# Attention transfers over all 128 partitions, outputs stored ahead of values, gate products later

## The chip, the cores and the metric

The kernel runs on one core of a Trainium2 chip. The metric is the device time of one execution in microseconds (us); lower is better. The profile is one execution recorded by the hardware profiler.

## The reference, cut to what matters

One layer of a diffusion backbone, for 2048 latent tokens and 256 context tokens of width 1024. An input projection yields q, k, v, a gate z_a, the inputs of a convolution branch, a gate z_b and two merge gates. Branch A is attention over a window of the latent grid plus context keys, 8 heads of width 64:

```
q, k, v, z_a, glu, z_b, gates = split(h @ w_in + b_in)
y_a = attend(q, k, v) * silu(z_a)
y_b = conv_branch(glu, ...) * silu(z_b)
g_a, g_b = split(sigmoid(gates))
m = g_a * (y_a @ w_proj_a) + g_b * (y_b @ w_proj_b)
return x + gate * (m @ w_out), k, v
```

Everything is float32. The kernel splits each factor of a product into a high and a low part, so that one product is three matmuls.

## The kernel before, in words

The program has three stages, one after another on TensorE: the input projection (the front), attention over the 8 heads, and the merge with the output projection (the tail). Results of the front go to DRAM (`proj`, `q_hi`, `q_lo`, `k_hi`, `k_lo`, `v`), and the attention loads them head by head.

A head has 18 tiles of 128 queries (`TPH`), so there are `NT` = 144 tiles. For a tile, TensorE forms the scores (`scores`), VectorE adds the bias and takes the minimum (`soften`), ScalarE takes exponents (`exponents`), TensorE transposes them (`turn_probs`) and for each pair of tiles multiplies by the values (`weigh_values`); VectorE multiplies the result by z_a and the inverse of the sum (`gate_out`).

The tiles that a head needs are doubled in SBUF (`n % 2`). `q_sp` (q_split in the profile) has the high part of q in partitions 0 to 63 and the low part in 64 to 127; `k_hi` and `k_lo` have the same 64 rows in both halves, so that one matmul over 128 partitions sums q_hi·k and q_lo·k. `z_sb` and `y_sb` (z_halves, y_halves) hold half of the tokens of a head in the lower 64 partitions and the other half in the upper 64.

All of these transfers are issued by SyncE (SP), in the order of its program. For heads 2 to 7 it issues `load_window` (8 transfers of 16 rows for the bias tables), `load_qk` (6), `load_z` (6), `load_v` (18) and `store_y` of head n - 2 (6). Each load waits until the head two before has let go of the buffer: `load_qk` for `s_mm` (scores done), `load_z` for `y_done`, `load_v` for `pv_done`. What is loaded for head 0 is issued during the front, between the stores of its last units (`load_first`).

```
        for n in range(2, HEADS):
            load_window(sp, n)
            load_qk(n)
            load_z(n)
            load_v(n)
            for part in range(3):
                store_y(sp, n - 2, part)
```

In the tail, `M_UNITS` lists the merge units; those of token chunk 0 (16 units of 256 tokens) come first. VectorE takes each unit out of its PSUM bank, multiplied by its gate (`g_done`), and TensorE may be six units ahead. Between them stand the operations of the convolution branch: `silu_pair` (ScalarE), `gate_yb` (VectorE, times z_b), `yb_high` (ScalarE) and `yb_low` (VectorE), for pairs 0, 1 and 2 of token tiles. Pair 0 belongs to chunk 0, pairs 1 and 2 to chunk 1, which begins with unit 16. z_b of pair 1 (`zb_second`) is loaded at the beginning of the tail.

Of the kernel before, what the change touches and what calls it, by code (L numbers as in the profile page):

```python
# [106 lines left out]
def modulation(nc, io, cst, hT_hi, hT_lo):  # L107
# [80 lines left out]
    io.gate = nc.dram_tensor("gate_rows_dram", (2, D), F32, kind="Internal").ap()  # L188
    io.q_hi, io.q_lo = (nc.dram_tensor(f"q_{h}_rows", (WA, TOK), F32, kind="Internal").ap() for h in ("hi", "lo"))
    io.k_hi, io.k_lo = (nc.dram_tensor(f"k_{h}_rows", (WA, KW), F32, kind="Internal").ap() for h in ("hi", "lo"))  # L190
# [747 lines left out]
def attend(nc, io, cst):  # L938
# [96 lines left out]

    def y_rows(n, half, part):

        rows = slice(DH * n, DH * n + DH)
        if part == 2:
            return rows, slice(LAT + P * half, LAT + P * half + P), slice(LAT // 2, LAT // 2 + P)  # L1040
        at = LAT // 2 * part + 512 * half
        return rows, slice(at, at + 512), slice(512 * part, 512 * part + 512)

    def store_y(sp, n, part):

        sp.wait_ge(y_done, PPH * n + Y_PARTS[part][1])
        for half in range(2):
            rows, tok, at = y_rows(n, half, part)
            sp.dma_start(io.ya[rows, tok], y_sb[DH * half:DH * half + DH, n % 2, at]).then_inc(y_out[n % 2], 16)

# [3 lines left out]
    def wait_y_stored(sp):  # L1054
        for u in range(2):
            sp.wait_ge(y_out[u], 96 * HEADS // 2)

# [15 lines left out]
    def _(sp):  # L1073
        def load_qk(n):

            if n >= 2:
                sp.wait_ge(s_mm, TPH * (n - 1))
            u, rows = n % 2, slice(DH * n, DH * n + DH)
            for half in range(2):
                part = slice(DH * half, DH * half + DH)  # L1080
                sp.dma_start(q_sp[u][part].bitcast(F32), (io.q_hi, io.q_lo)[half][rows]).then_inc(qk_in[u], 16)
                sp.dma_start(k_hi[u][part].bitcast(F32), io.k_hi[rows]).then_inc(qk_in[u], 16)
                sp.dma_start(k_lo[u][part].bitcast(F32), io.k_lo[rows]).then_inc(qk_in[u], 16)

# [28 lines left out]
        def load_z(n):  # L1113
            if n >= 2:
                sp.wait_ge(y_done, PPH * (n - 1))
            for half in range(2):
                for part in range(3):
                    rows, tok, at = y_rows(n, half, part)
                    src = io.proj[ZA0:ZA0 + WA][rows, tok]
                    sp.dma_start(z_sb[DH * half:DH * half + DH, n % 2, at], src).then_inc(z_in[n % 2], 16)  # L1120

# [8 lines left out]
        for n in range(2, HEADS):  # L1130
            load_window(sp, n)
            load_qk(n)
            load_z(n)
            load_v(n)
            for part in range(3):
                store_y(sp, n - 2, part)
        for done in (s_mm, pv_done, red):
            sp.wait_ge(done, TPH * (HEADS - 1))
# [4 lines left out]
        store_y(sp, HEADS - 1, 0)  # L1143
        sp.wait_ge(y_out[0], 96 * HEADS // 2)
        sp.wait_ge(y_out[1], 96 * (HEADS // 2 - 1) + 32)
        tail_stage.load_ya(sp, 0)
# [6 lines left out]
    def _(pe):  # L1153
        def scores(m):

            n, i = BODY[m]
            if m % TPH == 0:
                pe.wait_ge(qk_in[n % 2], 96 * (n // 2 + 1))
            if m >= 2:
# [85 lines left out]
    def _(dve):  # L1245
# [39 lines left out]
        def gate_out(k):  # L1285

            n, at = divmod(k, PPH)
            if at == 0:
                dve.wait_ge(z_in[n % 2], 96 * (n // 2 + 1))
                if n >= 2:  # L1290
                    dve.wait_ge(y_out[n % 2], 96 * (n // 2))
            dve.wait_ge(pv_done, 2 * k + 2)
# [29 lines left out]
    def _(act):  # L1322
# [33 lines left out]
        for m in range(NT + 1):  # L1356
            if 1 <= m < NT - 1:
                exponents(m + 1)
            if m < NT:
                copy_rest(m)  # L1360
                if m % 2:
                    spread(m // 2)
            tail_stage.early_act(act, m)
# [68 lines left out]
def tail(nc, io, cst):  # L1432
# [349 lines left out]
    def yb_high(act, lt):  # L1782

        src, c, tok = yb_parts(lt)
        act.wait_ge(yb_done, yb_count(lt))
        act.activation(y_hi[c][:, 4:8, tok], src, ACT.Copy).then_inc(yb_hid, 1)
# [37 lines left out]
    def tail_act(act):  # L1824
        for n, (c, o, branch) in enumerate(M_UNITS):
            s = n % 16
            if n == 1:
                yb_high(act, 2)
                silu_pair(act, 2)
            if n == 5:  # L1830
                yb_high(act, 4)
            if c == 4 and branch:
# [85 lines left out]
    def tail_dve(dve):  # L1918
        for n, (c, o, branch) in enumerate(M_UNITS):
# [21 lines left out]
            elif og > 32:  # L1941
                m_low(dve, og - 33)
            if n in (0, 4):
                gate_yb(dve, 2 + n // 2)
            if n in (2, 6):
                yb_low(dve, 2 if n == 2 else 4)
            for lt, a, b in turns(c):
# [72 lines left out]
    def early_dve(dve, m):  # L2020
# [10 lines left out]
        if m == NT:  # L2031
            gate_yb(dve, 0)
            yb_low(dve, 0)

    def early_act(act, m):
        for lt, d in pair_steps(m):
# [6 lines left out]
        if m == NT - 3:  # L2043
            ya_high(act, 0, 0)
            ya_high(act, 0, 1)
        if m == NT - 1:
            silu_pair(act, 0)
        if m == NT:
# [12 lines left out]
    T.early_pe, T.early_act, T.early_dve, T.early_pool = early_pe, early_act, early_dve, early_pool  # L2061
    T.lin_done = lin_done
    T.load_first, T.load_wp, T.load_ya = load_ln_first, load_wp, load_ya
# [80 lines left out]
```

## Time and profile before

| | us |
|---|---|
| median of 3 runs (1872.67 to 1877.26) | 1874.98 |
| the profiled execution | 1877.82 |
| its span, first to last instruction | 1875.6 |
| TensorE busy | 1829.8 (98%) |
| VectorE busy | 1015.1 (54%) |
| ScalarE busy | 542.0 (29%) |

The kernel is almost all TensorE. In the table "busy" is the time in which an engine has an instruction running; the rest of TensorE's span, 45.8 us, is idle time in all. The front takes the first 1150 us, attention ends at about 1460 us, the tail takes the rest.

### The profile page before, as it was taken

The numbers are of one execution on the slowest core, as the hardware profiler recorded it, in microseconds if no ns is written. First come the engines' busy times: TensorE is split into PE (matmuls) and PEld (weight loads), VectorE is DVE, ScalarE is ACT, GpSimd is POOL, SyncE is SP. The second block draws the span as 40 slices with busy tenths as digits, with TensorE's granted clock in tenths as the row PEclk, the third lists the DMA queues.
The fourth block names the chain that finished last, engine by engine and source line by source line (L and its number), as shares of the span: only waits on it lengthen the run. The fifth ranks groups of instructions, "written<-read, shape, count | busy, mean of one in ns | idle before, by whom it ended". The sixth has DMA issues, their size and how long they took to land.

```text
span 1875.6 us, 27263 instructions
## 1 busy us (share of the span) xinstructions
PE 1829.8 (98%) x10723; PEld 1561.1 (83%) x10723; DVE 1015.1 (54%) x1710; ACT 542.0 (29%) x1061; POOL 122.8 (7%) x205
## 2 busy tenths in 40 slices
PE   6999999999999999999999999999999899999998
PEld 3788899988888888888888888888888888888886
DVE  3544512111098338816870996766768555654444
ACT  3731101021111111211110114667768222322221
POOL 0100000000000000000000004322330000000000
PEclk9999999999999999999999999999999999999999
DMA  9524423143022112211220164997887767653321
GB/s 318 169 89 158 144 68 132 49 140 115 12 78 89 65 34 82 76 40 59 72 80 20 65 153 119 211 178 163 175 182 176 229 205 244 193 191 140 141 101 56
DMA packets 211145, 235.08 MB, mean 125 GB/s; under 512 B 47707, under 2 KB 157131, under 8 KB 207819
## 3 DMA queue, kind: packets, MB, share of 16 engines
q1 hardware_dynamic: 210760, 233.24, 42.5%
q8 instruction: 85, 1.39, 0.3%
q14 instruction: 41, 0.34, 0.1%
q10 hardware_dynamic: 259, 0.11, 0.0%
HBM read 152.52 MB, written 80.78 MB: 124 GB/s over the span
## 4 chain that ended last, share of the span: by engine, by line
PE 90%; SPq 4%; DMA 2%; issue 1%; ACT 1%; DVE 1%; POOLq 0%; DVEq 0%; POOL 0%; ACTq 0%
PE banks L789 17%; PE banks L790 17%; PE banks L791 17%; PE banks L1742 4%; PE banks L1741 4%; PE banks L1743 4%; PE banks L1713 3%; PE banks L1715 3%; PE banks L1714 3%; PE banks L1225 3%; SPq L1093 2%; PE banks L784 2%; PE banks L785 2%; PE banks L786 2%; PE banks L1191 2%
## 5 line engine op out<-in xcount | busy, mean ns | idle before, releaser
L789 PE MATMUL banks<-h_hi,w_hi 128*128 128x512 f32 (+1 forms) x1600 | 593.3, 371 | 3.6 <-DVE h_lo L598 2.5
L790 PE MATMUL banks<-h_lo,w_hi 128*128 128x512 f32 (+1 forms) x1600 | 589.4, 368 | 0.0
L791 PE MATMUL banks<-h_hi,w_lo 128*128 128x512 f32 (+1 forms) x1600 | 589.3, 368 | 0.0
L730 DVE SCALAR_TENSOR_TENSOR conv_acc<-glu_out,taps,conv_acc 128x773 f32<-128x773 f32 x360 | 371.5, 1032 | 12.3
L789 PEld LDWEIGHTS banks<-h_hi,w_hi 128*128 128x128 f32 x1600 | 301.8, 189 | 57.6 <-issue 3.4
L791 PEld LDWEIGHTS banks<-h_hi,w_lo 128*128 128x128 f32 x1600 | 301.8, 189 | 50.7
L790 PEld LDWEIGHTS banks<-h_lo,w_hi 128*128 128x128 f32 x1600 | 302.0, 189 | 49.0
L506 ACT ACTIVATE out_stage<-banks,param_cols 128x512 f32<-128x512 f32 (+1 forms) x120 | 77.0, 647 | 439.2 <-PE banks L791 433.2
L1713 PE MATMUL banks<-y_hi,wp_hi 128*128 128x512 f32 (+1 forms) x320 | 120.0, 375 | 4.9 <-DVE m_sum L1935 2.8
L1332 ACT ACTIVATE probs<-scores,stat 128x640 f32<-128x640 f32 (+2 forms) x128 | 106.7, 834 | 60.2 <-DVE stat L1259 58.6
L1715 PE MATMUL banks<-y_hi,wp_lo 128*128 128x512 f32 (+1 forms) x320 | 118.4, 370 | 0.0
L1714 PE MATMUL banks<-y_lo,wp_hi 128*128 128x512 f32 (+1 forms) x320 | 118.3, 370 | 0.0
L1742 PE MATMUL banks<-wo_lo,mo_hi 128*128 128x512 f32 x288 | 112.9, 392 | 0.0
L1741 PE MATMUL banks<-wo_hi,mo_hi 128*128 128x512 f32 x288 | 112.7, 391 | 0.0
L1743 PE MATMUL banks<-wo_hi,mo_lo 128*128 128x512 f32 x288 | 112.5, 391 | 0.0
L1259 DVE CUSTOM_DVE_ANT_0 scores<-banks,bias 128x640 f32<-128x640 f32 (+2 forms) x128 | 105.4, 824 | 11.4 <-PE banks L1169 10.9
L696 DVE SCALAR_TENSOR_TENSOR glu_out<-banks,param_cols,h_f 128x512 f32<-128x512 f32 (+1 forms) x20 | 14.0, 698 | 174.5 <-PE banks L791 174.5
L573 DVE SCALAR_TENSOR_TENSOR w_lo<-w_raw,w_hi 128x1024 fp32r<-128x1024 f32 x44 | 53.2, 1221 | 99.6 <-ACT w_hi L461 99.5
L1273 DVE COPY probs_t<-banks 96x256 f32<-96x256 f32 (+3 forms) x128 | 62.2, 486 | 66.0 <-PE banks L1191 66.0
L784 PE MATMUL banks<-w_hi,h_hi 128*128 128x256 f32 x288 | 81.7, 284 | 0.0
L786 PE MATMUL banks<-w_hi,h_lo 128*128 128x256 f32 x288 | 81.5, 283 | 0.0
L785 PE MATMUL banks<-w_lo,h_hi 128*128 128x256 f32 x288 | 81.5, 283 | 0.0
(161 smaller groups left out, 2397.5 us busy)
## 6 DMA issues: line engine op xcount, KB each, us to landing
proj<-out_stage SPq DMA_DIRECT2D x96, 256.0 KB, 2.0
w_raw<-in_w_in SPq DMA_DIRECT2D x44, 512.0 KB, 3.9
gates_in<-proj SPq DMA_DIRECT2D x64, 256.0 KB, 2.9
k_hi<-k_hi_rows SPq DMA_DIRECT2D x16, 640.0 KB, 13.2
k_lo<-k_lo_rows SPq DMA_DIRECT2D x16, 640.0 KB, 15.2
w_ada<-in_w_ada SPq DMA_DIRECT2D x8, 1024.0 KB, 10.8
x_out<-in_x_sample SPq DMA_DIRECT2D x16, 512.0 KB, 3.4
out_y_sample<-x_out SPq DMA_DIRECT2D x15, 512.0 KB, 2.6
```

The costliest lines, as they stand in the source:

```text
L730: op = dve.scalar_tensor_tensor(dst, src, tap, dst, ALU.mult, ALU.add)
L784: pe.matmul(out, h_hi[e][:, k, tok], w_hi[:, pair, k], start=first, stop=False)
L785: pe.matmul(out, h_hi[e][:, k, tok], w_lo[:, pair, k], start=False, stop=False)
L789: pe.matmul(out, w_hi[:, s, k], h_hi[c][:, k], start=first, stop=False)
L790: pe.matmul(out, w_hi[:, s, k], h_lo[c][:, k], start=False, stop=False)
L791: op = pe.matmul(out, w_lo[:, s, k], h_hi[c][:, k], start=False, stop=last)
L1713: pe.matmul(out, wp_hi[:, o, kk], y_hi[c][:, kk], start=(k == 0), stop=False)
L1714: pe.matmul(out, wp_hi[:, o, kk], y_lo[c][:, kk], start=False, stop=False)
L1715: last = pe.matmul(out, wp_lo[:, o, kk], y_hi[c][:, kk], start=False, stop=(k == 3))
L1741: pe.matmul(out, mo_hi[c][:, k, tok:tok + P], wo_hi[h][:, :, k], start=(k == 0), stop=False)
L1742: pe.matmul(out, mo_hi[c][:, k, tok:tok + P], wo_lo[h][:, :, k], start=False, stop=False)
L1743: last = pe.matmul(out, mo_lo[c][:, k, tok:tok + P], wo_hi[h][:, :, k], start=False, stop=(k == KC - 1))
```

## The change

Six edits. (1) q_hi and q_lo become the two halves of one DRAM tensor `q_both`, and a head's q_sp is loaded by one transfer of 128 partitions in place of two of 64. (2) k_hi and k_lo are each loaded by one transfer of 128 partitions whose source is the same 64 rows read twice (a step of 0), in place of two transfers of 64. (3) z_sb is loaded by three transfers in place of six. (4) y_sb is stored by three in place of six; `y_rows` gives the DRAM side as a pattern of three dimensions, half, row, token. (5) For heads 2 to 7 the stores of head n - 2 stand ahead of `load_v(n)`. (6) In the tail `gate_yb`, `yb_high` and `yb_low` of pairs 1 and 2 move from units 0 to 6 to units 4 to 10, and two `silu_pair` calls stand a little earlier. The bytes that are moved stay the same.

```
-    io.q_hi, io.q_lo = (nc.dram_tensor(f"q_{h}_rows", (WA, TOK), F32, kind="Internal").ap() for h in ("hi", "lo"))
+    io.q_both = nc.dram_tensor("q_rows", (2, WA, TOK), F32, kind="Internal").ap()
+    io.q_hi, io.q_lo = io.q_both[0], io.q_both[1]
...
-    def y_rows(n, half, part):
+    def y_rows(dram, n, part):
-        rows = slice(DH * n, DH * n + DH)
+        rows = dram[DH * n:DH * n + DH]
         if part == 2:
-            return rows, slice(LAT + P * half, LAT + P * half + P), slice(LAT // 2, LAT // 2 + P)
-        at = LAT // 2 * part + 512 * half
-        return rows, slice(at, at + 512), slice(512 * part, 512 * part + 512)
+            return rows[:, LAT:TOK].rearrange("p (h t) -> h p t", h=2), slice(LAT // 2, LAT // 2 + P)
+        at = LAT // 2 * part
+        return rows[:, at:at + LAT // 2].rearrange("p (h t) -> h p t", h=2), slice(512 * part, 512 * part + 512)
...
-        for half in range(2):
-            rows, tok, at = y_rows(n, half, part)
-            sp.dma_start(io.ya[rows, tok], y_sb[DH * half:DH * half + DH, n % 2, at]).then_inc(y_out[n % 2], 16)
+        dst, at = y_rows(io.ya, n, part)
+        sp.dma_start(dst, y_sb[:, n % 2, at]).then_inc(y_out[n % 2], 16)
...
-            for half in range(2):
-                part = slice(DH * half, DH * half + DH)
-                sp.dma_start(q_sp[u][part].bitcast(F32), (io.q_hi, io.q_lo)[half][rows]).then_inc(qk_in[u], 16)
-                sp.dma_start(k_hi[u][part].bitcast(F32), io.k_hi[rows]).then_inc(qk_in[u], 16)
-                sp.dma_start(k_lo[u][part].bitcast(F32), io.k_lo[rows]).then_inc(qk_in[u], 16)
+            twice = lambda k: k[rows].unsqueeze(0).to_broadcast([2, DH, KW])
+            sp.dma_start(q_sp[u][:].bitcast(F32), io.q_both[:, rows]).then_inc(qk_in[u], 16)
+            sp.dma_start(k_hi[u][:].bitcast(F32), twice(io.k_hi)).then_inc(qk_in[u], 16)
+            sp.dma_start(k_lo[u][:].bitcast(F32), twice(io.k_lo)).then_inc(qk_in[u], 16)
...
-            for half in range(2):
-                for part in range(3):
-                    rows, tok, at = y_rows(n, half, part)
-                    src = io.proj[ZA0:ZA0 + WA][rows, tok]
-                    sp.dma_start(z_sb[DH * half:DH * half + DH, n % 2, at], src).then_inc(z_in[n % 2], 16)
+            for part in range(3):
+                src, at = y_rows(io.proj[ZA0:ZA0 + WA], n, part)
+                sp.dma_start(z_sb[:, n % 2, at], src).then_inc(z_in[n % 2], 16)
...
             load_z(n)
-            load_v(n)
             for part in range(3):
                 store_y(sp, n - 2, part)
+            load_v(n)
...
-            if n == 1:
-                yb_high(act, 2)
+            if n == 0:
                 silu_pair(act, 2)
             if n == 5:
+                yb_high(act, 2)
+            if n == 9:
                 yb_high(act, 4)
...
-            if n in (0, 4):
-                gate_yb(dve, 2 + n // 2)
-            if n in (2, 6):
-                yb_low(dve, 2 if n == 2 else 4)
+            if n in (4, 8):
+                gate_yb(dve, n // 2)
+            if n in (6, 10):
+                yb_low(dve, n // 2 - 1)
```

The counts that are waited for on these semaphores are halved to match (96 to 48 for a head).

On SP's queue, one head of the attention loop stood so before (a row is line, operation, out<-in and the size of the side that is written; xN is N equal transfers in a row):

```order
L1069 DMA bias_window<-shifted_bias 16x752 x8
L1081 DMA q_split_99<-q_hi_rows 64x2304
L1082 DMA k_hi_100<-k_hi_rows 64x2560
L1083 DMA k_lo_101<-k_lo_rows 64x2560
L1081 DMA q_split_99<-q_lo_rows 64x2304
L1082 DMA k_hi_100<-k_hi_rows 64x2560
L1083 DMA k_lo_101<-k_lo_rows 64x2560
L1120 DMA z_halves<-proj 64x512 x2
L1120 DMA z_halves<-proj 64x128
...
L1093 DMA v_win_102<-v_tokens 24x8x64 x4
...
L1049 DMA ya<-y_halves 64x512 x4
L1049 DMA ya<-y_halves 64x128 x2
```

The same head in the changed kernel, on the same queue:

```order
L1069 DMA bias_window<-shifted_bias 16x752 x8
L1080 DMA q_split_99<-q_rows 128x1x2304
L1081 DMA k_hi_100<-k_hi_rows 128x1x2560
L1082 DMA k_lo_101<-k_lo_rows 128x1x2560
L1117 DMA z_halves<-proj 128x1x512 x2
L1117 DMA z_halves<-proj 128x1x128
L1049 DMA ya<-y_halves 2x64x512 x2
L1049 DMA ya<-y_halves 2x64x128
L1092 DMA v_win_102<-v_tokens 24x8x64 x4
L1092 DMA v_win_102<-v_tokens 32x8x64 x8
```

Nine transfers of 128 partitions stand where 18 of 64 stood, and the three stores are ahead of the values. The side in SBUF counts 128 partitions; the other side, in DRAM, is now a pattern that counts 2 on its outside and 64 rows in it, as the stores' rows show (2x64x512).

On VectorE at the beginning of the tail the product of pair 1 stood right after the first merge unit (rows with what they wait for):

```order
L1935 TENSOR_TENSOR m_sum<-banks,gates_in 128x256 [waits proj_mm,g_in0]
L1886 TENSOR_TENSOR cv_pair_146<-cv_pair_146,zb_second 128x1024 [waits zb1_in,act_pair]
L1935 TENSOR_TENSOR m_sum<-banks,gates_in 128x256 [waits proj_mm,g_in1]
L1935 TENSOR_TENSOR m_sum<-banks,gates_in 128x256 [waits proj_mm,g_in2]
L1892 TENSOR_TENSOR y_lo<-cv_pair_146,y_hi 128x4x256 [waits yb_hid]
```

In the changed kernel it reads so from the same first unit on (gated_b is the second branch of a unit, m_sum<-m_sum its addition):

```order
L1934 TENSOR_TENSOR m_sum<-banks,gates_in 128x256 [waits proj_mm,g_in0]
L1934 TENSOR_TENSOR m_sum<-banks,gates_in 128x256 [waits proj_mm,g_in1]
L1934 TENSOR_TENSOR m_sum<-banks,gates_in 128x256 [waits proj_mm,g_in2]
L1934 TENSOR_TENSOR gated_b<-banks,gates_in 128x256 [waits proj_mm]
L1938 TENSOR_TENSOR m_sum<-m_sum,gated_b 128x256 [waits gated]
L1934 TENSOR_TENSOR gated_b<-banks,gates_in 128x256 [waits proj_mm]
L1938 TENSOR_TENSOR m_sum<-m_sum,gated_b 128x256 [waits gated]
L1885 TENSOR_TENSOR cv_pair_146<-cv_pair_146,zb_second 128x1024 [waits zb1_in,act_pair]
```

The product is now behind the fifth unit, so that five units leave their banks before VectorE waits for zb_second.

## Rows read from the trace of the kernel before

**Rows 1.** The page, section 1: busy time of the whole span

```profile
PE 1829.8 (98%) x10723; PEld 1561.1 (83%) x10723; DVE 1015.1 (54%) x1710; ACT 542.0 (29%) x1061; POOL 122.8 (7%) x205
```

**Rows 2.** Busy time of each engine by stretch: attention, beginning of the tail

```profile
core 0: us, PE busy (x) PEld busy (x) DVE busy (x) ACT busy (x) POOL busy (x), PEclk, DMA share, GB/s
1150.00:1460.00 310.00, 297.48 (x2947) 265.24 (x2945) 217.69 (x643) 224.22 (x553) 75.34 (x107) 1.00 0.82 174
1460.00:1475.00 15.00, 11.03 (x83) 10.50 (x82) 7.71 (x13) 3.60 (x4) 0.00 (x0) 0.89 0.69 216
```

**Rows 3.** TensorE's waits from 1150 to 1480 us: total, times, longest

```profile
PE banks L1216 <- DMA v_ctx<-v_tokens: 2.6, 4, 1.2
PE banks L1216 <- DVE y_halves L1305: 2.3, 2, 1.4
PE banks L1166 <- DMA k_lo<-k_lo_rows: 0.9, 1, 0.9
```

**Rows 4.** SP's queue over one head, in order: start, time spent issuing

```profile
1236.47 3.82 SPq L1069 DMA_DIRECT2D bias_window<-shifted_bias  x8
1240.34 0.47 SPq L1081 DMA_DIRECT2D q_split<-q_hi_rows  x1
...
1244.58 3.79 SPq L1120 DMA_DIRECT2D z_halves<-proj  x6
1248.41 19.64 SPq L1093 DMA_DIRECT2D v_win<-v_tokens  x16
...
1269.04 4.38 SPq L1049 DMA_DIRECT2D ya<-y_halves  x6
1273.46 0.58 SPq L1069 DMA_DIRECT2D bias_window<-shifted_bias  x1
```

**Rows 5.** Stretches with one kind of transfer: x rows, tables, keys, values

```profile
51.00:54.00 3.00, 3.00 (x15) 2.48 (x14) 2.14 (x4) 1.04 (x2) 1.34 (x2) 1.00 1.02 419
64.00:67.00 3.00, 3.00 (x17) 2.47 (x16) 0.49 (x1) 2.90 (x7) 0.00 (x0) 1.00 0.49 50
1244.00:1247.00 3.00, 3.00 (x30) 2.73 (x27) 1.84 (x9) 1.84 (x6) 2.92 (x5) 1.00 1.00 205
1227.00:1232.00 5.00, 4.75 (x44) 4.08 (x41) 3.23 (x11) 3.79 (x10) 0.00 (x0) 1.00 0.74 135
```

**Rows 6.** The page, DMA issues: count, KB each, median us to landing

```profile
w_raw<-in_w_in SPq DMA_DIRECT2D x44, 512.0 KB, 3.9
...
k_hi<-k_hi_rows SPq DMA_DIRECT2D x16, 640.0 KB, 13.2
...
q_split<-q_hi_rows SPq DMA_DIRECT2D x8, 576.0 KB, 5.1
...
v_win<-v_tokens SPq DMA_DIRECT2D x64, 64.0 KB
z_halves<-proj SPq DMA_DIRECT2D x32, 128.0 KB, 17.2
...
v_win<-v_tokens SPq DMA_DIRECT2D x64, 48.0 KB
...
bias_window<-shifted_bias SPq DMA_DIRECT2D x64, 47.0 KB, 2.0
...
z_halves<-proj SPq DMA_DIRECT2D x16, 32.0 KB, 17.2
```

**Rows 7.** SP's queue from 48 us, and the landing of that w_raw

```profile
49.18 5.78 SPq L342 DMA_DIRECT2D shifted_bias<-table_pad  x16
55.01 0.40 SPq L289 DMA_DIRECT2D w_raw<-in_w_in  x1
...
DMA to landing us min/median/max: 15.6/15.6/15.6
```

**Rows 8.** SP's queue near the end of the front, head 0's loads

```profile
1099.36 0.53 SPq L1081 DMA_DIRECT2D q_split<-q_hi_rows  x1
...
1104.14 11.20 SPq L372 DMA_DIRECT2D proj<-out_stage  x3
...
1119.14 7.35 SPq L1093 DMA_DIRECT2D v_win<-v_tokens  x16
```

**Rows 9.** VectorE at the beginning of the tail, with its idle time before

```profile
1468.91 1.23 DVE L1886 TENSOR_TENSOR cv_pair<-cv_pair,zb_second 128x1024 f32<-128x1024 f32 x1 [4.93 <-DMA zb_second<-proj]
```

More of the change, by code:

```diff
@@ L1055, in wait_y_stored @@
         for u in range(2):
-            sp.wait_ge(y_out[u], 96 * HEADS // 2)
+            sp.wait_ge(y_out[u], 48 * HEADS // 2)
     io.wait_bank, io.store_last_y, io.wait_y_stored, io.wait_ln_bank = wait_bank, store_last_y, wait_y_stored, wait_ln_bank
@@ L1143, in _ @@
         store_y(sp, HEADS - 1, 0)
-        sp.wait_ge(y_out[0], 96 * HEADS // 2)
-        sp.wait_ge(y_out[1], 96 * (HEADS // 2 - 1) + 32)
+        sp.wait_ge(y_out[0], 48 * HEADS // 2)
+        sp.wait_ge(y_out[1], 48 * (HEADS // 2 - 1) + 16)
         tail_stage.load_ya(sp, 0)
@@ L1157, in scores @@
             if m % TPH == 0:
-                pe.wait_ge(qk_in[n % 2], 96 * (n // 2 + 1))
+                pe.wait_ge(qk_in[n % 2], 48 * (n // 2 + 1))
             if m >= 2:
@@ L1288, in gate_out @@
             if at == 0:
-                dve.wait_ge(z_in[n % 2], 96 * (n // 2 + 1))
+                dve.wait_ge(z_in[n % 2], 48 * (n // 2 + 1))
                 if n >= 2:
-                    dve.wait_ge(y_out[n % 2], 96 * (n // 2))
+                    dve.wait_ge(y_out[n % 2], 48 * (n // 2))
             dve.wait_ge(pv_done, 2 * k + 2)
@@ L1360, in _ @@
                 copy_rest(m)
+                tail_stage.early_silu(act, m)
                 if m % 2:
@@ L2033, in early_dve, with early_silu @@
             yb_low(dve, 0)
+    def early_silu(act, m):
+        if m == NT - 1:
+            silu_pair(act, 0)
     def early_act(act, m):
@@ L2045, in early_act @@
             ya_high(act, 0, 1)
-        if m == NT - 1:
-            silu_pair(act, 0)
         if m == NT:
@@ L2061, in tail @@
     T.early_pe, T.early_act, T.early_dve, T.early_pool = early_pe, early_act, early_dve, early_pool
-    T.lin_done = lin_done
+    T.lin_done, T.early_silu = lin_done, early_silu
     T.load_first, T.load_wp, T.load_ya = load_ln_first, load_wp, load_ya
```

## The prediction

> **What bounds the kernel now.** I read first the page's busy times [rows 1]: TensorE is at work for 1829.8 of 1875.6 us, so only a stage in which it idles can give anything back. The view of engines by stretch shows where the changed transfers lie [rows 2]. In attention (1150 to 1460 us, 38.8 us a head) TensorE is busy for 297.5 of 310 us, so 12.5 us are idle; in the first 15 us of the tail it is busy for 11.0, so 4.0 are idle. At most 16.5 us are therefore to be had from all six edits. The waits of TensorE name transfers in a few places: 2.6 us for the values, 0.9 for keys, and 2.3 for an output product that stood behind a store [rows 3].
>
> SP's own queue is the second reading. One head's turn goes from 1236.47 to 1273.46, 37.0 us, and it is busy issuing all that time [rows 4]: 19.6 us of it go into the 16 transfers of v_win, whereas the same 16 took 7.35 us when head 0's were issued [rows 8]. SP is held up because the DMA engines are full: their share in attention is 0.82 [rows 2]. So attention stands on an edge. TensorE needs some 37 us a head, and so do the transfers. What the change does to the rate of a transfer decides.
>
> **What the transfers run at.** Three stretches show three rates [rows 5]. Rows of x into 128 partitions: 419 GB/s at a share of 1.02, or 26.2 GB/s for each of the 16 engines. Keys into 64 partitions: 205 GB/s at a share of 1.00, or 12.8 each: all engines are busy and each is at half speed. That is what the edit is after. Tables out of 8 partitions: 50 GB/s at a share of 0.49. Here half of the engines did nothing, though the queue was not empty: the 16 table stores (eight rows each) were issued by 54.96 and a weight load at 55.01, and the latter landed 15.6 us later, where its kind takes 3.9 [rows 6, 7]. So a transfer whose pattern counts 8 on its outside was carried by 8 of the 16 engines, and a later transfer's pieces on those engines had to queue behind it.
>
> The changed transfers are of a kind that no row of before has. One side counts 128 partitions, the other counts 2 on its outside (two halves, each of 64 rows). If the split over engines must fit both sides, as the table rows suggest for their eight, two engines carry each of these transfers. If the side in SBUF alone decides, or the halves are flattened into rows, 16 do. I take two engines, since the nearest row, the tables, followed the outer count down and left the rest idle.
>
> The Trainium skill, "DMA: Bandwidth & Descriptors", section "Why a DMA increments its semaphore by 16 and not by 1", says that a DMA runs on the largest number of engines up to 16 that divides the slowest dimension (of size over 1) of both sides, which is 2 here; its rules for kernel authors warn of a leading broadcast of few copies. By its figure of about 27 GiB/s for an engine, an estimate of the q and k load below would be 3.80 MB / 58 GB/s = 66 us in place of 72.5. That it is 8 for the tables agrees with the share of 0.49. The same page's rules also speak for the change: two transfers to disjoint halves should be one of 128 partitions. By that rule alone the result would be that of the first rival.
>
> **The cost of the transfers on two engines.** Bytes of a head [rows 6]: q is 2 x 576 KB, k_hi and k_lo 2 x 640 KB each, together 3712 KB = 3.80 MB. z is 4 x 128 + 2 x 32 = 576 KB = 0.59 MB, and y as much. The rest stays spread: v_win 8 x 64 + 8 x 48 KB, 128 KB of context values (two transfers of 128 x 2 x 64 elements) and 8 x 47 KB of windows, 1400 KB = 1.43 MB, which at the values' pace (135 GB/s at a share of 0.74, so 182 at 1) is 8 us of every engine.
>
> Two engines, each writing to its own half of the partitions, are little in each other's way, so I give each 26.2 GB/s, together 52.4. The other end is 12.8 each. q and k: 3.80 MB / 52.4 = 72.5 us. z: 11.3 us. y: 11.3 us. With the spread part, a head costs the two engines 72.5 + 11.3 + 8 = 91.8 us, and 103.1 where a y is stored too. That is against 37 us of work for TensorE. SP's waits don't add to it: load_qk(n), load_z(n), the stores and load_v(n) wait for head n - 2, and its 37 us are over well inside a batch of 103. So the two engines never run dry, and their work sets the end of attention.
>
> The sum: head 0's first load is issued at 1099.4 [rows 8]. Eight heads and six y are 8 x 91.8 + 6 x 11.3 = 802 us. In the same queues run the front's last stores and the tail's first loads, about 6 MB over all engines at 419 GB/s, 15 us; latency and the one point where SP waits for all of the front's stores, some 6 us. The values of head 7 are there at 1099 + 802 + 21 = 1922. TensorE is then two tiles in, and needs some 36 us for the rest: attention ends at 1958 instead of 1460, +498. The front is held up too (proj stores behind head 0's 72.5 us [rows 8]), but that lies under the same 1922. **Predicted: 1877.8 + 498 - 4 = 2372** for the profiled execution, which is 2.8 above the median; so 2370.
>
> **Edits 5 and 6.** Stores ahead of the values move three stores past 18 transfers. The gain is that y_done of head n - 2 is met sooner, whose trace is the 2.3 us wait; behind them load_v waits for nothing new, as y_done and pv_done of a head come together. On two engines the stores also push the values back by 11.3 us, which is in the sum in either order. The gate products: VectorE sat 4.93 us waiting for zb_second [rows 9] with finished merge units behind it, and TensorE, six units ahead, ran out of banks. Behind the fifth unit that wait is covered, and pair 1 is wanted only with unit 16. The silu calls do the same work elsewhere. I take 4 us off, of 4.0 idle [rows 2]; from 0 to 4 is possible.
>
> **The rivals.**
> - *The transfers spread over all 16 engines*: faster. The rows for 64 partitions and for x say that this would double the rate, and SP's 19.6 us for v_win would fall toward 7.35. TensorE's idle time would shrink by the waits on transfers and stores (2.6 + 0.9 + 2.3, say 6 of 12.5) and the 4 of the tail: 1875 - 10 = 1865, at best 1875 - 16.5 = 1858. It holds from seven engines on: 4.98 MB / (k x 26.2) + 8 is under 38.8 us when k is over 6.2. Against it: nothing but the tables' rows and the missing row of its own kind.
> - *Two engines at 12.8 each*, as the keys run now: q, k, z and y take twice as long, 8 x 175.6 + 6 x 22.5 = 1540, or 738 more: about 3110. The keys' rate comes from 16 engines sharing 64 partitions, which two don't; so I hold it unlikely, and a mild slowdown (10 to 25% on the 802, up to 2570) likelier.
> - *Only the side that is read decides*: the loads are on two engines, the stores spread. Then 6 x 11.3 = 68 us go: 2302. If only the written side decides, the loads are spread and the stores take 11.3 us of a 38.8 us head, hidden: as the first rival.
> - *Two engines, but hidden*, since loads are two heads ahead: no. A lead of two heads hides a delay, not a lower rate, and 91.8 us a head are over twice what 38.8 allows.
>
> **Chances.** Two engines near their full rate, 0.74; with stores spread, 0.04; with a mild slowdown, 0.06; slower still, 0.03; spread over 16, 0.12; some other way, 0.01. The range 2295 to 2600 holds the first three and a little more than the 8 in 10 wanted. A measurement here can tell about 0.2% from no change (the three runs of before span 0.24%). Faster by more than that is the first rival's 0.12, less a little for no gain: 0.11. Same: 0.02. Slower: 0.87.
>
> **What would show it.** k_hi's median landing goes from 13.2 us to over 50. The DMA share of attention falls from 0.82 to about 0.2 (two engines of 16 full, the rest 8 of 103 us), and the rate from 174 to some 62 GB/s. TensorE waits about 65 us a head, in front of the scores or the inverse's transpose (L1216), released by q, k or v transfers, and is busy for some 36% of attention. Head 2's to head 7's loads follow each other at 103 us. VectorE no longer waits for zb_second ahead of the second merge unit. The prediction is wrong if k_hi lands within 15 us (then two engines was wrong), or if it lands late with heads at another distance than 103 us (then the rate was).

## The result, and the profile after

The changed kernel takes 2413.0 us (median of 4 runs, 2410.9 to 2416.0); the kernel before, run beside it, 1875.8. The ratio is 1.287, with an interval of 1.285 to 1.289: 537 us slower. The profiled execution took 2415.96 us, its span is 2413.8.

The page of the changed kernel, busy time of the whole span and one of the DMA issues (count, KB each; to be read beside [rows 1, 6]):

```profile
PE 1870.2 (77%) x10723; PEld 1595.4 (66%) x10723; DVE 1013.2 (42%) x1710; ACT 543.3 (23%) x1061; POOL 119.9 (5%) x205
...
k_hi<-k_hi_rows SPq DMA_DIRECT2D x8, 1280.0 KB
```

Busy time by stretch, of the changed kernel, same columns as [rows 2]: attention from 1200 us on, the beginning of the tail, and a stretch in which only q and k are moved:

```profile
1200.00:1996.00 796.00, 323.99 (x2869) 286.98 (x2870) 216.11 (x638) 220.72 (x546) 75.48 (x107) 0.70 0.20 67
1996.00:2010.00 14.00, 14.00 (x121) 13.66 (x120) 6.58 (x13) 3.39 (x4) 0.00 (x0) 0.97 0.55 162
...
1530.00:1590.00 60.00, 23.16 (x243) 20.73 (x241) 16.79 (x54) 17.64 (x45) 7.73 (x11) 0.72 0.13 54
```

The last row is the whole result in small. The DMA share is 0.13, which is 2 of 16, and the rate 54 GB/s, 27 for each of two engines, where the keys of before ran at 205 with a share of 1.00 [rows 5]. Attention as a whole went from a share of 0.82 and 174 GB/s [rows 2] to 0.20 and 67, and TensorE is busy for 41% of it.

TensorE's waits from 1050 to 2100 us (total, times, longest), to be read beside [rows 3]:

```profile
PE banks L1163 <- DMA k_lo<-k_lo_rows: 336.0, 7, 53.4
PE banks L1213 <- DMA v_ctx<-v_tokens: 127.7, 7, 20.6
PE banks L790 <- ACT out_stage L507: 39.5, 1, 39.5
```

A head waits once for its keys and once for its values, 66 us together ((336.0 + 127.7) / 7). The third row is the front, held up behind head 0's loads.

SP's queue of the changed kernel, head 3's q and k at 1417.93 and then the whole turn of head 4, to be read beside [rows 4]:

```profile
1417.93 0.54 SPq L1080 DMA_DIRECT2D q_split<-q_rows  x1
...
1521.52 4.75 SPq L1069 DMA_DIRECT2D bias_window<-shifted_bias  x8
1526.31 0.54 SPq L1080 DMA_DIRECT2D q_split<-q_rows  x1
...
1527.45 19.60 SPq L1082 DMA_DIRECT2D k_lo<-k_lo_rows  x1
1547.09 54.28 SPq L1117 DMA_DIRECT2D z_halves<-proj  x3
1601.41 12.72 SPq L1049 DMA_DIRECT2D ya<-y_halves  x3
1614.18 13.32 SPq L1092 DMA_DIRECT2D v_win<-v_tokens  x16
...
1628.49 4.38 SPq L1069 DMA_DIRECT2D bias_window<-shifted_bias  x8
```

SP issues a k_lo load in 19.6 us and three z loads in 54.3: each issue takes as long as the two engines need to make room. From window to window a head takes 107.0 us (1521.52 to 1628.49), where it took 37.0.

TensorE of the changed kernel, the first scores of head 3 and the place at which head 7's values had landed (start, duration, what ended the idle time before):

```profile
1492.31 0.61 PE L1163 MATMUL banks<-k_hi,q_split 128*128 128x288 f32 x1 [45.58 <-DMA k_lo<-k_lo_rows]
...
1952.57 0.47 PE L1213 MATMUL banks<-ident,inv_wide 128*128 128x128 f32 x1 [18.75 <-DMA v_ctx<-v_tokens]
1952.97 1.55 PE L1222 MATMUL banks<-probs_t,v_win 96*64 96x128 f32 x12
...
1960.00 0.88 PE L1222 MATMUL banks<-probs_t,v_win 128*64 128x128 f32 x12
```

Head 3's q load was issued at 1417.93 and its last key landed at 1492.3: 74.4 us. The last two rows are twelve products each, of 128 columns, in 1.55 and in 0.88 us. The stretch before them, in which TensorE had nothing to do:

```profile
1943.00:1952.00 9.00, 0.00 (x0) 0.00 (x0) 0.00 (x0) 0.00 (x0) 0.00 (x0) 0.50 0.52 122
```

The granted clock is 0.50 there, the 1.2 GHz level, and TensorE starts head 7's values at it; at 1960 it is at 2.4 GHz again.

VectorE at the beginning of the tail, to be read beside [rows 9]:

```profile
2007.01 1.23 DVE L1885 TENSOR_TENSOR cv_pair<-cv_pair,zb_second 128x1024 f32<-128x1024 f32 x1 [0.72 <-DMA zb_second<-proj]
...
2014.13 0.42 DVE L1934 TENSOR_TENSOR m_sum<-banks,gates_in 128x256 f32<-128x256 f32 x1 [5.10 <-DMA gates_in<-proj]
```

The wait for zb_second fell from 4.93 to 0.72 us, and seven microseconds later VectorE stands 5.10 us in front of the gates of a later merge unit.

### The profile page after: what moved, and what is told of

Read it like the earlier page. It is cut to its first block, busy times and chain, and to the rows that moved or that the text cites. A ratio compares the mean times of both kernels' runs of the same rounds, so it can differ in the third digit from the quotient of the medians.

```text
span 2413.8 us, 27191 instructions
## 1 busy us (share of the span) xinstructions
PE 1870.2 (77%) x10723; PEld 1595.4 (66%) x10723; DVE 1013.2 (42%) x1710; ACT 543.3 (23%) x1061; POOL 119.9 (5%) x205
## 4 chain that ended last, share of the span: by engine, by line
PE 70%; another core or an unknown queue 14%; SPq 9%; DMA 3%; issue 1%; DVE 1%; ACT 1%; POOL 0%; POOLq 0%; DVEq 0%; ACTq 0%
PE banks L790 13%; PE banks L791 13%; PE banks L792 13%; SPq L1092 4%; PE banks L1222 4%; PE banks L1739 3%; PE banks L1740 3%; PE banks L1741 3%; PE banks L1711 3%; PE banks L1713 3%; PE banks L1712 3%; SPq L1117 2%; PE banks L1188 1%; PE banks L785 1%; PE banks L786 1%
## 5 line engine op out<-in xcount | busy, mean ns | idle before, releaser
L1163 PE MATMUL banks<-k_hi,q_split 128*128 128x384 f32 (+2 forms) x128 | 58.3, 455 | 336.0 <-DMA k_lo<-k_lo_rows 336.0
L1163 PEld LDWEIGHTS banks<-k_hi,q_split 128*128 128x128 f32 x128 | 26.4, 206 | 337.6 <-DMA k_lo<-k_lo_rows 337.6
L1213 PE MATMUL banks<-ident,inv_wide 128*128 128x128 f32 x72 | 22.0, 306 | 127.9 <-DMA v_ctx<-v_tokens 127.7
L1339 ACT ACTIVATE probs_t<-banks 128x384 f32<-128x384 f32 x144 | 67.6, 469 | 172.2 <-PE banks L1194 171.9
L1213 PEld LDWEIGHTS banks<-ident,inv_wide 128*128 128x128 f32 x72 | 10.6, 148 | 129.5 <-DMA v_ctx<-v_tokens 129.1
```

## The experiments

Each ratio is against the kernel before on the same chip, with its 95% interval. Lines of waits and of stretches have the columns shown above.

**The q and k loads alone (edits 1 and 2).** Before, with

```
+            twice = lambda k: k[rows].unsqueeze(0).to_broadcast([2, DH, KW])
+            sp.dma_start(q_sp[u][:].bitcast(F32), io.q_both[:, rows]).then_inc(qk_in[u], 16)
+            sp.dma_start(k_hi[u][:].bitcast(F32), twice(io.k_hi)).then_inc(qk_in[u], 16)
+            sp.dma_start(k_lo[u][:].bitcast(F32), twice(io.k_lo)).then_inc(qk_in[u], 16)
```

> The kernel before with edits 1 and 2 alone: q, k_hi and k_lo of a head each by one transfer of 128 partitions whose source counts 2 halves on its outside; z and y as before, in 64 partitions. Theory (two engines carry a transfer that counts 2 on its outside): the q and k cluster of a head stays at 72.5 us as in the changed kernel; the rest of a head is what it was there (107.2 - 72.5 = 34.7 us) less the 22.6 us of z and y on two engines plus about 6 us for the same bytes spread, so 18 us; a head every 90 us, and about 17 us x 7.5 heads = 125 us less than the changed kernel: 2290 us. Rival (the loss comes mostly from z and y, whose rows are short and strided, and q and k are hidden two heads ahead): under 1950 us.

Measured: 2298.1 us, 1.225 [1.223, 1.227]. TensorE's waits for keys, and one stretch with q and k alone:

```profile
PE banks L1166 <- DMA k_lo<-k_lo_rows: 367.7, 7, 54.0
```

```profile
1316.00:1340.00 24.00, 5.99 (x69) 5.25 (x65) 4.24 (x15) 5.37 (x17) 0.00 (x0) 0.67 0.13 55
```

These loads carry 422 of the 537 us, and their share is 0.13 again. The theory's 2290 was 8 us short.

**z and y alone (edits 3 and 4).** Before, with `y_rows` giving `rearrange("p (h t) -> h p t", h=2)` and three loads and three stores a head.

> The kernel before with edits 3 and 4 alone: z and y by transfers of 128 partitions with an outer count of 2 on the DRAM side, q and k as before. Theory: on the two engines a head costs 18.5 us for q and k (3.80 MB at 205 GB/s), 8 us for values and windows, 23 us for z and y and some 5 us in which SP issues windows: 54 us against 38.8 us a head, so about +15 us x 8 = 120 us: near 2000 us. If two engines carry only a transfer whose source counts 2, y is spread and a head costs 42 us: about 1900 us. Rival (z and y are small enough to hide): 1870 to 1880 us.

Measured: 1982.2 us, 1.057 [1.055, 1.059]. TensorE's two longest waits:

```profile
PE banks L1213 <- DVE y_halves L1302: 44.8, 6, 8.0
PE banks L1213 <- DMA v_ctx<-v_tokens: 32.6, 7, 8.2
```

This tells whether the stores are confined too. With the stores spread, the two engines would have 18.5 us of keys and q (3.80 MB at 205 GB/s), 11.3 of z and 8 of the rest, 37.8 a head, and TensorE's 38.8 would still set the pace. With the stores on two engines it is 49.1. In the trace the q loads of the heads with stores follow each other at 50.4 to 51.9 us, so the stores are confined. A stretch of this kernel right behind the issue of a head's three stores shows it directly:

```profile
1257.00:1261.00 4.00, 2.32 (x19) 2.01 (x16) 0.63 (x2) 0.71 (x2) 0.00 (x0) 1.00 0.13 51
```

The share is 2 of 16 for stores as well: the side that is written decides as well as the side that is read. The two losses, 422 and 106, make 528 of 537.

**The same transfers, rows outside.** As the first experiment, with the two dimensions of the DRAM side exchanged: 64 rows outside, the two halves inside. Same bytes, same number of transfers, same 128 partitions. Both sides are walked in this order, so partition 2r of q_sp gets the high part of row r and 2r + 1 the low one, and k_hi and k_lo hold row r in both. The scores are sums over all 128 partitions and stay the same.

```
-            twice = lambda k: k[rows].unsqueeze(0).to_broadcast([2, DH, KW])
-            sp.dma_start(q_sp[u][:].bitcast(F32), io.q_both[:, rows]).then_inc(qk_in[u], 16)
+            twice = lambda k: k[rows].unsqueeze(1).to_broadcast([DH, 2, KW])
+            sp.dma_start(q_sp[u][:].bitcast(F32), io.q_both[:, rows].rearrange("h p t -> p h t")).then_inc(qk_in[u], 16)
```

> The kernel before with q, k_hi and k_lo each by one transfer of 128 partitions, but with the rows outside and the two halves inside the source pattern (64 rows x 2 halves), so that partition 2r holds the high part of row r of q and 2r + 1 the low part, and k's row r stands in both. The same bytes, the same repeated rows, the same 128 partitions as in the changed kernel. Theory (the outer count deals a transfer out, and 64 is a multiple of 16): all 16 engines carry it, at up to 419 GB/s, 9 us a head in place of 18.5; attention is bound by TensorE, and some of its 12.5 us of idle time go: 1865 to 1874 us. Rival (the repeated source, the size of one transfer or 128 partitions are to blame): as slow as e1, near 2290 us.

Measured: 1867.2 us, 0.9955 [0.9943, 0.9968]: faster than before by 8 us (6 to 11), where the other order of the same two dimensions lost 422. The page's k_hi row (with its median landing), a stretch with q and k alone, and attention:

```profile
k_hi<-k_hi_rows SPq DMA_DIRECT2D x8, 1280.0 KB, 8.7
```

```profile
1298.00:1303.00 5.00, 4.75 (x43) 4.09 (x43) 4.39 (x14) 3.07 (x8) 4.92 (x7) 1.00 1.01 428
...
1150.00:1460.00 310.00, 301.15 (x2995) 269.73 (x2993) 220.42 (x648) 225.39 (x553) 75.32 (x107) 1.00 0.64 180
```

428 GB/s at a full share, twice the 205 of before. TensorE's waits on keys, values and stored y [rows 3] are gone, and the share of attention fell from 0.82 to 0.64, so there is slack now. The Trainium skill, "DMA: Bandwidth & Descriptors", in its rules for kernel authors, asks for one transfer of 128 partitions in place of two to disjoint halves; that this gains holds here only with 64 on the outside.

**Four and eight on the outside.** The transfers of before, of 64 partitions, with the 64 rows dealt so that the pattern counts 4 or 8 outside. The order of the rows is another, the same for q and k, and scores don't depend on it. The first kernel's edit (a=8 in the second):

```
+            dealt = lambda d: d[rows].rearrange("(b a) t -> a b t", a=4)
-                sp.dma_start(k_hi[u][part].bitcast(F32), io.k_hi[rows]).then_inc(qk_in[u], 16)
+                sp.dma_start(k_hi[u][part].bitcast(F32), dealt(io.k_hi)).then_inc(qk_in[u], 16)
```

> The kernel before with its 64-partition transfers of q, k_hi and k_lo, but with the 64 rows of each read in another order: 4 on the outside, 16 inside (row a + 4b lands in partition 16a + b, the same in both halves and for q and k). The same bytes, the same 6 transfers. Theory (the outer count of one side sets the number of engines when it is under 16): four engines carry q and k, 3.80 MB / (4 x 26.2) = 36.3 us a head; with 6 us of z and y, 8 of values and windows, 5 of SP's issuing, 55 us a head against 38.8: about +16 us x 7.5, near 2000 us. Rival (what counts is that the source is not one block of rows, or the size of transfers; not the count of 2): either no change or as slow as e1.

> As e5, with 8 on the outside and 8 inside. Theory: eight engines carry q and k, 18.1 us a head at 26.2 GB/s each, which is what 16 engines take for the same 64 partitions (18.5 us at 205 GB/s). On those eight engines a head costs 18.1 + 6 + 8 + 5 = 37 us: at the edge of the 38.8 us, so 1874 to 1890 us. Rival as in e5: as slow as e1, or equal to e5.

Measured: four, 2073.5 us, 1.105 [1.102, 1.108]; eight, 1979.8 us, 1.055 [1.052, 1.057]. Of each, the longest of TensorE's waits and a stretch of q and k; first of four:

```profile
PE banks L1167 <- DMA k_lo<-k_lo_rows: 174.2, 7, 28.6
```

```profile
1312.00:1318.00 6.00, 5.72 (x55) 5.12 (x54) 4.74 (x13) 3.35 (x9) 2.24 (x6) 1.00 0.25 73
```

And of eight:

```profile
PE banks L1167 <- DMA k_lo<-k_lo_rows: 93.3, 7, 16.1
```

```profile
1336.00:1346.00 10.00, 9.59 (x103) 8.51 (x99) 6.53 (x24) 6.93 (x19) 0.00 (x0) 1.00 0.53 114
```

The shares, 0.25 and 0.53, are the counts, 4/16 and 8/16. The rates are not in proportion: 73 / 4 = 18 GB/s an engine and 114 / 8 = 14, where two engines had 27 each and my expectations took 26. For four this is only a part of the story. Later in the same head the same loads run at another rate:

```profile
1335.00:1343.00 8.00, 0.00 (x0) 0.00 (x0) 0.00 (x0) 0.00 (x0) 0.00 (x0) 0.50 0.25 107
```

That is 27 GB/s for each of four engines, with one pattern and one set of partitions. TensorE stood still in that stretch; whether this matters was not tried. For eight, four stretches in three heads lie between 114 and 121 GB/s, 14 to 15 an engine. So the number of engines follows the outside count, and the rate of one engine is not set by the pattern alone. Both expectations missed, four by 73 us and eight by 90. A cause is only argued here. The Trainium skill, "SBUF — State Buffer", section "Door 1: The DMA port swizzle", says that 4 neighbouring partitions and the 4 that are 32 further share a port. Eight engines that each walk 8 rows would then meet in pairs; the 114 to 121 GB/s of eight fit that. Four that each walk 16 rows would meet in pairs too, which fits neither the 73 well nor the 107 at all unless they fall out of step, and no run here separates the ports.

**Windows behind q and k.** The changed kernel with `load_window(sp, n)` moved from ahead of `load_qk(n)` to behind it.

> The changed kernel with one swap for heads 2 to 7: the q and k loads are issued ahead of the eight window loads in place of behind them. In the changed kernel a head takes 107.2 us where the prediction had 103.1. Theory: the missing 4 us are SP's. It is held up while the two engines carry z, y and values, gets free only when they are nearly done, and then issues eight window loads (4.4 us) before the next q load, so the two engines run dry for about that long once a head. With the swap, six heads lose some 4.4 us each: 2413 - 26 = about 2387, and head follows head at about 103 us. Rival: the two engines have no gap and the extra 4 us are a lower rate of z and y (written or read beside the spread transfers): then the swap changes nothing, 2413 within 5, and heads stay 107 us apart.

Measured: 2402.6 us, 1.281 [1.279, 1.284], 10.5 less than the changed kernel. Stretches at the end of a head in the changed kernel:

```profile
1619.00:1624.00 5.00, 0.00 (x0) 0.00 (x0) 0.00 (x0) 0.00 (x0) 0.00 (x0) 0.50 0.38 102
1624.00:1628.00 4.00, 0.00 (x0) 0.00 (x0) 0.00 (x0) 0.00 (x0) 0.00 (x0) 0.50 0.60 136
1628.00:1633.00 5.00, 2.88 (x23) 2.61 (x23) 0.00 (x0) 0.00 (x0) 0.00 (x0) 0.50 0.44 110
```

SP's queue in this kernel, where the q loads of two heads stand, and then its stretches at the end of that head:

```profile
1515.70 0.54 SPq L1080 DMA_DIRECT2D q_split<-q_rows  x1
...
1620.83 0.54 SPq L1080 DMA_DIRECT2D q_split<-q_rows  x1
```

```profile
1612.00:1617.00 5.00, 0.00 (x0) 0.00 (x0) 0.46 (x2) 1.64 (x5) 0.00 (x0) 0.98 0.46 113
1617.00:1621.00 4.00, 0.00 (x0) 0.00 (x0) 0.00 (x0) 0.00 (x0) 0.00 (x0) 0.50 0.55 124
```

Both theories were half right. A head now takes 105.1 us (1515.70 to 1620.83), 2 less; the swap was to give 4.4. What stays is in the last rows: while the 18 loads of the values are issued, the share is 0.46 and 0.55, so for some 9 us the engines as a whole are not full. The share doesn't say which of them idle; that the two are among them is inferred. With windows ahead of q, that stretch is 14 us long (0.38 to 0.60). So the gap is not the windows' alone: their place is worth 2 us a head, though the stretch became some 5 us shorter. That the rest is SP's issuing of the values was not tried. TensorE's waits mostly changed their name: those for keys fell from 336.0 to 191.9 us and those for values from 127.7 to 47.8, while 189.3 were added in front of VectorE's transposed probabilities, since the tables now came last.

**Stores ahead of the values, alone (edit 5).** Before, with `load_v(n)` behind the three `store_y`.

> Before with edit 5 alone: the stores of head n - 2 are issued ahead of the values of head n. Theory: 0 to 2 us, since TensorE's waits on a stored y were 2.3 us and on values 2.6 us in all, so 1874 to 1877, no difference that can be measured. Rival: the values come later by the stores' work (0.59 MB at 174 GB/s, 3.4 us a head) on queues that have no slack, and TensorE waits for v_ctx: 6 x 2 us or so, 1885 to 1890.

Measured: 1872.5 us, 0.9982 [0.9973, 0.9991], 3.4 us faster (1.7 to 5.1). All that is left of TensorE's waits on transfers and stores:

```profile
PE banks L1216 <- DMA v_ctx<-v_tokens: 1.9, 1, 1.9
...
PE banks L1166 <- DMA k_lo<-k_lo_rows: 0.7, 1, 0.7
```

The wait behind a stored y (2.3 us [rows 3]) is gone and the values' fell from 2.6 to 1.9: 3.0 in these rows, the size of the gain. I had expected no difference that can be measured. The later values cost nothing.

**The gate products alone (edit 6).** Before, with the lines of the diff in `tail_act` and `tail_dve`, and the earlier silu.

> The kernel before with edit 6 alone: gate products, high and low parts of pairs 1 and 2 later in chunk 0 of the merge, silu calls a little earlier; no transfer is changed. Theory: VectorE no longer waits 4.9 us for zb_second ahead of the second merge unit and TensorE's idle time of 4.0 us at the beginning of the tail goes: 4 us less, about 1872 us. Rival (the wait moves to another unit or to pair 2's product, which comes later now): no change, within 1 us of 1876.

Measured: 1877.9 us, 1.0006 [0.9997, 1.0015]. VectorE, and the first 40 us of the tail, the first row of them to be read beside [rows 2]:

```profile
1480.59 0.42 DVE L1937 TENSOR_TENSOR m_sum<-banks,gates_in 128x256 f32<-128x256 f32 x1 [7.05 <-DMA gates_in<-proj]
```

```profile
1460.00:1475.00 15.00, 14.61 (x128) 14.21 (x127) 7.72 (x14) 4.58 (x6) 0.00 (x0) 1.00 0.62 171
1475.00:1500.00 25.00, 20.08 (x115) 17.86 (x114) 14.86 (x27) 3.85 (x4) 0.79 (x2) 0.93 0.70 228
```

The next 25 us, and what ended TensorE's two idle times in the first 15, in the kernel before:

```profile
1475.00:1500.00 25.00, 25.00 (x158) 22.50 (x158) 15.14 (x30) 4.05 (x5) 0.79 (x2) 1.00 0.85 282
...
1461.96 0.38 PE L1713 MATMUL banks<-y_hi,wp_hi 128*128 128x256 f32 x1 [1.19 <-DVE y_lo L1892]
1470.62 0.35 PE L1713 MATMUL banks<-y_hi,wp_hi 128*128 128x256 f32 x1 [2.78 <-DVE m_sum L1935]
```

Of the 4.0 us of idle time 3.6 left the first 15 us (14.61 busy for 11.03), and 4.9 came up in the next 25, which had none. VectorE's wait for zb_second is down to 0.43 us, and instead it stands in front of the gates. Only 2.78 of the 4.0 had stood behind a merge unit at all; the other 1.19 were a wait for the low part of pair 0.

**Its silu back, and then the gates earlier.** First the earlier silu of pair 0 is put back behind the last inverse; then also the gates of unit 3 are issued ahead of SP's wait for the stored y.

```
-                tail_stage.early_silu(act, m)
...
+        load_gates(sp, 3)
```

> e4 with the first silu call back behind the last spread of the inverses (its place before the change); the gate products stay later. Theory formed from e4's trace: the table load and silu of 2.3 us now stood ahead of the last inv_wide, which held back the last output product, its store, the load of y for chunk 1 behind that store, and the gates of unit 6 behind that load. With the silu back, 1 to 2 us less than e4: 1876. Rival (only the gate loads' place in SP's queue counts): as e4, 1878.

> e7, and SP issues the fourth pair of gate loads (merge unit 6) ahead of its wait for the last stores and of the 1 MB load of y for chunk 1. Theory: in e4 VectorE's wait of 4.9 us for zb_second had turned into one of 7.1 us for these gates, because SP could issue them only behind the wait and the load; with both out of the way TensorE's 4 idle us at the beginning of the tail go: 1872. Rival (the tail has further waits of the same kind behind this one, so that it moves again): 1876.

Measured: 1878.5 us, 1.0014 [1.0003, 1.0024], and 1876.6, 1.0004 [0.9993, 1.0014]. Neither gave the 4 us, and the first not even the 1 to 2 us that I had expected against the gate products alone; it is 0.6 to 4.5 us slower than before. In the second, VectorE's waits for gates were cut up and not gone, six of them with 3.6 us the longest, and TensorE's longest wait is now one for a low part of y:

```profile
DVE m_sum L1937 <- DMA gates_in<-proj: 9.4, 6, 3.6
...
PE banks L1714 <- DVE y_lo L1899: 3.2, 2, 2.3
```

**The change with its transfers right.** Rows outside for q and k, z and y as before, edits 5 and 6; then the same with the silu back and the gates first.

> The changed kernel's q and k loads with the 64 rows on the outside of the pattern and the two halves inside, z and y as before (six transfers each), and edits 5 and 6. Theory: the gain of the row order alone, 8 us, and nothing from edits 5 and 6: 1866 to 1869. Rival: with the queues relieved the stores' earlier place and the later gates add their 2 and 4 us: 1860 to 1863.

> The previous kernel, with the silu of pair 0 back behind the sums' inverse on ScalarE and the gates of merge unit 3 issued ahead of the wait for the stored y. Theory: as the row order alone, 1865 to 1868, because the idle time at the beginning of the tail only moved from one wait to the next in the two kernels that had these edits without the row order. Rival: with the queues relieved all gates arrive in time and the 4 us of idle time in the tail's first 15 us go: 1861 to 1864.

Measured: 1870.4 us, 0.9974 [0.9962, 0.9985], and 1867.2, 0.996 [0.9946, 0.9973]. The row of TensorE's longest wait in the tail of the first:

```profile
PE banks L1714 <- DVE m_sum L1937: 4.9, 1, 4.9
```

The first is by its median 3 us above the row order alone, with intervals that touch, and its TensorE waits 4.9 us for a merge unit that waits for its gates. VectorE's longest wait for gates is 7.5 us there and 2.6 us in the second kernel, which comes out level with the row order alone, 1867.2 for both. So with the transfers right, edits 5 and 6 add nothing that shows: the waits that edit 5 shortened are gone with the faster keys alone, and edit 6 needs two more edits to cost nothing. The version to keep is the third experiment's. Rows outside for z and y as well were not tried.

## Why the prediction was right, and where it was off

**Two engines: right.** The step "the split over engines must fit both sides" is shown by the row order: 2 outside gives a share of 0.13, 64 outside 1.00 and more, with the same bytes, transfers and partitions (only which row lands in which partition differs), and 4 and 8 give 0.25 and 0.53. The rival with all 16 engines falls for this pattern, and is what happens for the other. Its 1865 is within 3 us of the 1867.2 measured, in part by luck: it counted 4 us of edit 6, which that kernel doesn't have and which gave nothing. The rival "only the side that is read decides" (2302) falls by the second experiment.

**What was to be seen.** The sign named for k_hi, a median landing of over 50 us, can't be read: the page gives none. Worked out from its bytes and q's, 2.49 MB at 54 GB/s, it landed some 47 us after its issue, a little under the sign; the last key, k_lo, landed 74 us after the first load was issued. The share of attention is 0.20 for about 0.2 and the rate 67 for 62; waits of 66 us a head for 65; TensorE busy for 41% of attention, for 36; 107 us a head for 103.

**26.2 GB/s an engine: right.** A head's q and k took 72 to 74 us from their first to their last packet, against 72.5. The rival at 12.8 an engine falls. I had called it unlikely since two engines can't crowd 64 partitions; the run with 8 outside shows that the half rate comes back when eight engines write to 64 partitions (14 to 15 GB/s each), and with 4 outside it came and went within a head (18 to 27).

**The head: 107 us, not 103.1.** The term that was mis-sized is the 8 us for what is spread. For z and y I had 22.6 us, and they took some 21, from 1598 to 1619:

```profile
1598.00:1618.00 20.00, 9.81 (x70) 8.47 (x70) 6.28 (x19) 6.42 (x16) 0.00 (x0) 0.76 0.13 49
```

From 1619 to 1633 values and windows took 14 us, at shares of 0.38 to 0.60 (rows of the changed kernel under the windows' experiment). The step that failed is "the two engines never run dry". SP's 37 us are indeed well inside a head, but they are not free to lie anywhere: SP is held in front of the z and y transfers until the engines have room, and the 26 small transfers behind them are issued only when the two have little left. Some 2 us of the 4 were shown to be the windows; that the others are the values stays argued. Six heads by some 4 us are about 25 of the 30.6 us by which head 7's values were late (1952.6 for 1922), and the other 6 lie before head 2.

**The end of attention: 1998, not 1958.** Beside the 30.6, the last 18 tiles took 45.3 us from head 7's first inverse to its last, for the 36 I had given them. Rows of before, the same two places, and then of the changed kernel:

```profile
1421.93 0.27 PE L1216 MATMUL banks<-ident,inv_wide 128*128 128x128 f32 x1
1459.91 0.27 PE L1216 MATMUL banks<-ident,inv_wide 128*128 128x128 f32 x1
```

```profile
1990.60 0.69 PE L1194 MATMUL banks<-ident,probs 128*128 128x128 f32 x2 [3.81 <-ACT probs L1329]
1997.89 0.27 PE L1213 MATMUL banks<-ident,inv_wide 128*128 128x128 f32 x1
...
1991.00:1997.00 6.00, 6.00 (x31) 6.00 (x30) 2.46 (x5) 4.55 (x6) 0.00 (x0) 0.52 0.08 21
```

Before, this stretch took 38.0 us, so 2 of the 9 are a mis-sized term. About 3 are the clock: from the first inverse to the second it is 7.2 us (1952.57 to 1959.80), most of it at half the clock, where before it was 4.1. The rest came at the very end. ScalarE stood 3.10 us in front of the first y of the merge before it took the last exponents, TensorE was idle for 3.81 us behind them, and its clock then fell to 0.52 once more.

**Edit 5: right in kind**, 3.4 us for the 2.3 named. In the changed kernel it is of no account beside the waits of 66 us a head.

**Edit 6: wrong.** "Behind the fifth unit that wait is covered" held: 0.7 us for 4.93. That the 4 us would come off the total did not. From attention's last product with the values (1998) to the end (2413.8) it is 415.8 us, and before it was 415.6 (1460 to 1875.6). Of the 4.0 us that I booked, 1.19 had nothing to do with zb_second. The step left out was what is late next: the gates of unit 3 and later come by the same queue, behind SP's wait for the stored y and everything issued after it, and with VectorE no longer late it is they that are. The gates also have only three buffers, so that such a load waits for VectorE as well; more buffers were not tried. As far as these runs show, the early part of the tail is bound by when its loads land, and edits that move VectorE's work inside it move the wait.

**The sum** for the profiled execution was 2372, and it took 2416. Of these 44 us, 30.6 are the heads, 9 the last tiles, 4 the edit that gave nothing.

## What to carry to other kernels

Read a transfer's pattern from its outside: with 2, 4 or 8 there, as many engines were at work here, and with 64 all 16. It holds for the side that is read and for the side that is written, and 128 partitions on the other side didn't help. If one transfer is to replace two to the halves of SBUF, let the rows be the outer count and the halves the inner one; for q and k that is 8 us gained for 422 lost. And where a stage is fed by many loads, a consumer's wait that is covered is worth its length only if the next load behind it is in time; look that one up before the gain is booked.

## What the runs showed of the hardware

- The rate of one engine is not a constant. Two engines, each into its own half of the partitions, ran at 27 GB/s; four at 18 to 27 (73 and 107 GB/s in two stretches of one head) and eight at 14 to 15, into 64 partitions dealt in blocks of 16 and 8; sixteen at 12.8 into 64 [rows 5] and at 26.7 into 128 (428 / 16).
- SP is held at a transfer when its engines are full: 43.59 us at one z load in the changed kernel, and 46.99 at three stores of the front, which held up ScalarE's staging and by it TensorE (39.5 us). A transfer on two engines so delays work that has nothing to do with it.
- TensorE's granted clock fell to 0.50 (1.2 GHz) in the waits and its mean over attention was 0.70. Its busy time rose from 1829.8 to 1870.2 us for the same 10723 instructions. Most of it lies under the transfers and costs nothing; some 3 us at the start of head 7's last tiles did cost.
